# Gate stage: low parts and full copies on VectorE, one kind of sums on GpSimd, sums behind the gate units, no weight slot left out

## The reference

```python
def rmsnorm(x, w):
    xf = x.astype(jnp.float32)
    y = xf * lax.rsqrt(jnp.mean(xf * xf, axis=-1, keepdims=True) + EPS)
    return (y * w.astype(jnp.float32)).astype(x.dtype)

def first_block(x, ...):
    ...
        mix = jnp.concatenate([att, ssd, gdn], axis=-1) @ w_out[l]
        x = x + rmsnorm(mix, post_mix_norm[l])
        h = rmsnorm(x, pre_ffn_norm[l])
        f = (jax.nn.silu(h @ ffn_w_gate[l]) * (h @ ffn_w_up[l])) @ ffn_w_down[l]
        x = x + rmsnorm(f, post_ffn_norm[l])
```

## Time and profile before

| what | value |
|---|---|
| median of 3 runs | 2189.01 us |
| time of the profiled execution | 2190.16 us |
| its span, first to last instruction | 2188.0 us |
| mean granted TensorE clock | 0.983 |
| TensorE busy | 2077.9 us (95%) |
| VectorE busy | 1291.4 us (59%) |
| ScalarE busy | 952.2 us (44%) |
| GpSimd busy | 991.2 us (45%) |
| the gate stage touched here | about 656 to 745 us |
| the 20 groups of seven | about 730 to 1111 us |

### The profile page before, as it was taken

One profiled execution on the slowest core, in us unless ns is written; L12 is line 12 of the kernel. 1 busy time (PEld: TensorE's weight loads), 2 busy tenths in 40 slices (PEclk: granted clock), 3 DMA queues, 4 the chain that ended last, 5 costly groups with the idle time before them and its releaser, 6 DMA issues. The chain is left out here.

```text
span 2188.0 us, 30026 instructions
## 1 busy us (share of the span) xinstructions
PE 2077.9 (95%) x10677; PEld 1752.7 (80%) x10685; DVE 1291.4 (59%) x1872; ACT 952.2 (44%) x1691; POOL 991.2 (45%) x723
## 2 busy tenths in 40 slices
PE   7999999889998999999999988889999999999997
PEld 7888877778786788888888867769998888887886
DVE  4443604867347734434379797789997864225532
ACT  4333215566224434343445654248884445444011
POOL 2333434544246688888840312210003469885344
PEclk9999999999999999999999999999999999999999
DMA  5233412353622122222244424210001111333331
GB/s 164 77 98 110 144 54 48 66 130 54 159 58 90 29 57 68 77 68 77 68 159 147 147 85 138 97 30 1 1 1 34 39 36 46 113 97 106 106 125 77
DMA packets 185892, 179.49 MB, mean 82 GB/s; under 512 B 27556, under 2 KB 147088, under 8 KB 184336
## 3 DMA queue, kind: packets, MB, share of 16 engines
q1 hardware_dynamic: 157568, 107.51, 16.9%
q10 hardware_dynamic: 19216, 46.99, 5.8%
q0 software_dynamic: 8960, 23.07, 4.8%
HBM read 150.81 MB, written 49.81 MB: 92 GB/s over the span
## 5 line engine op out<-in xcount | busy, mean ns | idle before, releaser
L1222 POOL TENSOR_SCALAR w_hi<-w_raw 128x1024 fp32r<-128x1024 f32 x67 | 76.3, 1138 | 465.6 <-issue 309.5
L1364 PE MATMUL gemm<-h_hi,w_hi 128*128 128x512 f32 x688 | 271.4, 395 | 5.5 <-POOL h_lo L1276 5.5
L1366 PE MATMUL gemm<-h_hi,w_lo 128*128 128x512 f32 x688 | 268.1, 390 | 0.0
L1365 PE MATMUL gemm<-h_lo,w_hi 128*128 128x512 f32 x688 | 267.8, 389 | 0.0
L968 POOL TENSOR_TENSOR w_lo<-wsum,w_hi 128x512 fp32r<-128x512 f32 x160 | 214.5, 1341 | 100.2 <-ACT w_hi L1841 92.1
L1841 ACT ACTIVATE w_hi<-wsum 128x512 fp32r<-128x512 f32 x171 | 108.2, 633 | 184.0 <-POOL wsum L959 97.7
L968 POOL TENSOR_TENSOR w_lo<-w_raw,w_hi 128x512 fp32r<-128x512 f32 x86 | 117.5, 1366 | 137.9 <-ACT w_hi L1841 133.5
L1225 POOL TENSOR_TENSOR w_lo<-w_raw,w_hi 128x1024 fp32r<-128x1024 f32 x67 | 166.2, 2481 | 5.6
L1446 PE MATMUL gemm<-h_hi,w_hi 128*128 128x512 f32 x416 | 162.0, 390 | 0.7 <-issue 0.7
L1448 PE MATMUL gemm<-h_hi,w_lo 128*128 128x512 f32 x416 | 161.8, 389 | 0.0
L1447 PE MATMUL gemm<-h_lo,w_hi 128*128 128x512 f32 x416 | 161.8, 389 | 0.0
(11 more groups left out here) (494 smaller groups left out, 5366.8 us busy)
## 6 DMA issues: line engine op xcount, KB each, us to landing
w_raw<-in_w_in SPq DMA_DIRECT2D x60, 512.0 KB, 4.0
down_sums<-in_ffn_w_down POOLq DMA_DIRECT2D x24, 768.0 KB, 7.2
w_raw<-in_ffn_w_gate SPq DMA_DIRECT2D x22, 512.0 KB, 4.0
w_raw<-in_ffn_w_up SPq DMA_DIRECT2D x22, 512.0 KB, 4.1
w_raw<-down_sums SPq DMA_DIRECT2D x44, 256.0 KB, 2.7
w_raw<-in_ffn_w_down SPq DMA_DIRECT2D x44, 256.0 KB, 2.9
w_raw<-in_w_out SPq DMA_DIRECT2D x16, 512.0 KB, 3.8
sig_spill<-quad ACTq DMA_DIRECT2D x5, 1024.0 KB, 3.9
```

What stands on the lines that cost most here:

```text
L1222: gp.tensor_scalar(hi[:], raw[key % 4][:], 1.0, 0.0, ALU.mult, ALU.add).then_inc(pool_hi, 1)
L1364: mm(o, hi[:, k, m], act[0][:, k, t], start=k == 0, stop=False)
L1365: mm(o, hi[:, k, m], act[1][:, k, t], start=False, stop=False)
L1366: last = mm(o, lo[:, k, m], act[0][:, k, t], start=False, stop=k == kt - 1)
```

## The change

- In `norm` (1, 0) and (1, 1) VectorE makes the low part straight from the side bank, as in the other norms, with `low` (L2275). GpSimd's low parts (L1276) and their semaphore are gone, and TensorE's gate units no longer wait for them.
- The full copies are a new item `full`: VectorE adds `h_hi` and `h_lo` in SBUF, 8 operations for the first token half, then 4 and 4 for the second, set between the sums.
- `csum` 3 is made by GpSimd, once eight sums of kinds 1 and 0 are there. ScalarE's high parts of this kind wait for a semaphore of its own.
- `csum` and `comb` 1 no longer stand ahead of the gate units' second halves but behind them, as all others. The order behind the gate units is `full` 0, kind 1, `full` 1, kind 0, `csum` 3 (GpSimd), `full` 2, kind 2, unit up 0, `csum` 4, unit up 1, `comb` 3, `comb` 4. VectorE has no work in a gate unit, so in its queue kind 1 keeps its place; ScalarE made the high parts of kind 1 ahead of the gates' silu (L1823) and makes them behind it now.
- The row sums (`rows` (0, 1)) stand behind `norm` (1, 0), and the four residuals as an item of their own behind them; before, the residuals were mixed into the norm's copies. The second store of x1 (`load` 7) stands behind the squares and the diagonals.
- `at_slot` leaves out no slot ahead of a group of seven.

```diff
--- before.py
+++ after.py
@@ -250,11 +250,12 @@
     s += [("mx", 0)] + tk("wo", (0, 0, 0), (0, 1, 0)) + [("gn", len(NORMED) - 1), ("mx", 1), ("load", 0)]
     s += tk("wo", (0, 0, 1), (0, 1, 1), (0, 2, 0), (0, 2, 1), (0, 3, 0), (0, 3, 1))
     s += tk("wo", (1, 0, 0), (1, 1, 0), (1, 2, 0), (1, 3, 0)) + [("rows", (0, 0)), ("resid", (0, 0)), ("nsq", (1, 0))]
-    s += tk("wo", (1, 0, 1), (1, 1, 1), (1, 2, 1), (1, 3, 1)) + [("rows", (0, 1))]
+    s += tk("wo", (1, 0, 1), (1, 1, 1), (1, 2, 1), (1, 3, 1))
     begin([("gate", 0), ("gate", 1)],
-          [("norm", (1, 0)), ("load", 6), ("load", 7), ("nsq", (1, 1))],
-          [("norm", (1, 1)), ("csum", 1), ("comb", 1)])
-    s += [("csum", 0), ("comb", 0), ("csum", 2), ("comb", 2), ("csum", 4), ("csum", 3), ("unit", by["up", 0]), ("unit", by["up", 1]), ("comb", 3), ("comb", 4)]
+          [("norm", (1, 0)), ("load", 6), ("rows", (0, 1)), ("resid", (0, 1)), ("nsq", (1, 1)), ("load", 7)],
+          [("norm", (1, 1))])
+    s += [("full", 0), ("csum", 1), ("comb", 1), ("full", 1), ("csum", 0), ("comb", 0), ("csum", 3), ("full", 2), ("csum", 2), ("comb", 2)]
+    s += [("unit", by["up", 0]), ("csum", 4), ("unit", by["up", 1]), ("comb", 3), ("comb", 4)]
     for p in range(1, NF // 2):
         s += [("mul", (by["gate", 2 * p], i)) for i in range(7)]
         s += [("mul", (by["up", 2 * p], i)) for i in range(7)]
@@ -426,7 +427,6 @@
             at_slot += at_slot % 2
         elif kind == "mul":
             key, width, user = j, 1, j
-            at_slot += j[1] == 0
         elif kind == "dm":
             key, width, user = ("dm",) + j, 1, ("dm",) + j
             at_slot += j == (0, 0)
...
@@ -888,10 +888,6 @@
             if q < 3:
                 return x, y, op, bsum[k][:], [cmb[q][i][:, k, :] for i in range(2)]
             return (x, y, op) + ((b21, mul_operand(5, k)) if q == 3 else (b12, mul_operand(6, k)))
-
-        def comb_source(eng, q, k):
-
-            side_consumed(eng, (("norm", (1, int(q != 1))), k + 4 * (q != 4)))
 
         def comb_low(eng, q, k):
 
@@ -1261,6 +1257,11 @@
                         pool.wait_ge(N["sq_part"], 16 + 8 * t + 4 * h + 2 * pair + 2)
                         x = acc[:, 4 * t + 2 * pair:4 * t + 2 * pair + 2, 512 * h:512 * h + 512]
                         step(gp.tensor_tensor(x, x, over(gbc2[:, 512 * h:512 * h + 512], 2), ALU.mult), "acc_gained")
+                elif kind == "csum" and j == 3:
+                    pool.wait_ge(N["comb_sum"], 8)
+                    for k in range(4):
+                        x, y, op, dst, _ = comb_of(3, k)
+                        step(gp.tensor_tensor(dst, x, y, op), "comb_sum_p")
                 elif kind == "c2":
                     (r1, t1), (r2, t2), op = pair_of(j // 4, j % 4)
                     if j == 0:
@@ -1269,11 +1270,6 @@
                     if j >= 2:
                         pool.wait_ge(N["c2_s"], j - 1)
                     step(gp.tensor_tensor(wt[j % 2][:], hF[1][:, r1, t1], hF[1][:, r2, t2], op), "c2_w")
-                elif kind == "norm" and j[0] == 1:
-                    t = slice(512 * j[1], 512 * j[1] + 512)
-                    for k in range(KD):
-                        side_consumed(pool, (it, k))
-                        step(gp.tensor_tensor(hT[1][:, k, t], hfull[:, k, t], hT[0][:, k, t], ALU.subtract), "low_ready")
                 elif kind == "pa":
                     c, z = j, j % 2
                     if c == 0:
@@ -1359,8 +1355,6 @@
                     for k in range(kt):
                         if kd in act_ready:
                             norm_consumed(pe, act_ready[kd](hf), k)
-                        if kd == ("gate", 0):
-                            pe.wait_ge(N["low_ready"], 8 * hf + k + 1)
                         mm(o, hi[:, k, m], act[0][:, k, t], start=k == 0, stop=False)
                         mm(o, hi[:, k, m], act[1][:, k, t], start=False, stop=False)
                         last = mm(o, lo[:, k, m], act[0][:, k, t], start=False, stop=k == kt - 1)
@@ -1939,8 +1933,10 @@
                     for k in range(4):
                         if j in (2, 4):
                             act.wait_ge(N["comb_add"], 4 * (j == 4) + k + 1)
+                        elif j == 3:
+                            act.wait_ge(N["comb_sum_p"], k + 1)
                         else:
-                            act.wait_ge(N["comb_sum"], 4 * (1, 0, 3).index(j) + k + 1)
+                            act.wait_ge(N["comb_sum"], 4 * (1, 0).index(j) + k + 1)
                         _, _, _, x, dst = comb_of(j, k)
                         step(af(dst[0], x, ACT.Copy), "comb_hi")
                 elif kind == "tk":
@@ -2520,14 +2516,16 @@
                     down_evict(*j)
                     if j[0] in CLOSING and j[1] > 0:
                         last_gain(j[1] - 1)
-                elif kind == "csum" and j in (0, 1, 3):
+                elif kind == "full":
+                    t = slice(512 * (j > 0), 512 * (j > 0) + 512)
+                    for k in (range(8), range(4, 8), range(4))[j]:
+                        step(v.tensor_tensor(hfull[:, k, t], hT[0][:, k, t], hT[1][:, k, t], ALU.add))
+                elif kind == "csum" and j < 2:
                     for k in range(4):
-                        comb_source(dve, j, k)
                         x, y, op, dst, _ = comb_of(j, k)
                         step(v.tensor_tensor(dst, x, y, op), "comb_sum")
-                elif kind == "csum":
+                elif kind == "csum" and j != 3:
                     for k in range(4):
-                        comb_source(dve, j, k)
                         x, y, op, dst, _ = comb_of(j, k)
                         step(v.tensor_tensor(dst, x, y, op), "comb_add")
                         if j == 2 and k > 0:
@@ -2570,14 +2568,7 @@
                     for k in range(KD):
                         b = side_product(dve, (it, k))
                         g0 = 64 + 8 * stage + k
-                        if stage == 1:
-                            hi_count[0] += 1
-                            dve.wait_ge(N["hi_ready"], hi_count[0])
-                            step.frees(v.tensor_scalar(hfull[:, k, t], b[:], cols[:, g0:g0 + 1], None, ALU.mult), (it, k))
-                        else:
-                            low(hT[1][:, k, t], b[:], hT[0][:, k, t], (it, k), cols[:, g0:g0 + 1])
-                        if stage == 1 and hf == 0 and k % 2:
-                            residual(stage - 1, 4 + k // 2)
+                        low(hT[1][:, k, t], b[:], hT[0][:, k, t], (it, k), cols[:, g0:g0 + 1])
                 elif kind == "nk":
                     hi_count[0] += 1
                     dve.wait_ge(N["hi_ready"], hi_count[0])
```

More of the change, by code:

```diff
@@ L727, in build_program @@
             "ln_sq", "c2_w", "c2_s", "c2_hi", "c2_lo", "idr_ready", "quad_ready",
-            "low_ready", "acc_gained", "comb_sum", "comb_add", "comb_hi", "comb_lo", "w_sum", "w_quarter_hi", "t_copied", "sg_ready", "f_made", "tok_used", "ob_sq", "ob_gained")}
+            "acc_gained", "comb_sum", "comb_sum_p", "comb_add", "comb_hi", "comb_lo", "w_sum", "w_quarter_hi", "t_copied", "sg_ready", "f_made", "tok_used", "ob_sq", "ob_gained")}
         z_out = [sem(f"z_out{i}") for i in range(2)]
```

## The result

| | before | after |
|---|---|---|
| median, timed side by side (19 runs each) | 2189.96 us (2187.16 to 2195.57) | 2195.64 us (2192.68 to 2197.21) |
| span of the profiled execution | 2188.0 us | 2191.6 us |
| mean granted clock | 0.983 | 0.979 |

The ratio is 1.0015, with an interval of 1.0009 to 1.0021: 2.0 to 4.6 us slower, and within 0.5%. Why the two measures differ by 2 us is not settled. The kernel before itself spreads widely: of its 31 executions timed beside slots_only, the 16 with a mean granted clock of 0.978 or 0.979 took 2190.9 to 2195.6 us, the eight at 0.982 or 0.983 took 2188.1 to 2189.7 us. For the other kernels the ratio is given, with its interval.

What follows compares the result with a forecast made beforehand. VectorE's queue from second norm to first eviction was the bound: 678.3 + 10.7 + 50.6 + 8.7 + 1.8 + 0.8 puts the sixth product at 750.9 against 744.42, 6.5 us later. Median 2195.5 us, eight in ten 2186 to 2202.

Steps and rivals of the forecast that it cites:

- Step 1: At the second norm: it starts at 678.3 instead of 683.90, 5.6 us gained, behind 3.8 us of TensorE idle.
- Step 2: In the second norm: half clock behind the wait costs 1.6 us, counted once, here.
- Step 3: VectorE's queue: 12 more operations cost 8.7 us, contention 1.8 us more (20.9 instead of 19.1).
- Step 4: Up units and products: first product at 729.9 behind a 10 us wait, second at 737.9, 5.3 us late.
- Step 5: Slots ahead of groups of seven: weights may start one product (2.72 us) sooner, gaining and costing nothing; later stages shift unchanged.
- A: Rival at the gate stage: TensorE-bound, VectorE's work covered, sixth product 11.1 us earlier, 2177.9 us; chance 0.06.
- B: Rival in VectorE's queue: less contention, 9.7 us instead of 20.9, 2184.3 us; up to +3 us, chance 0.2.
- C: Rival at the products: half clock through four products from 737.9, +15.3 us, 2204.3 us; chance 0.05.
- D: Rival in VectorE's queue: more contention, GpSimd working without a break, +13.7 us, 2202.7; chance 0.05 with its second form.
- D's second form: VectorE's queue: contended operations wait for GpSimd's whole instruction, 1.29 us instead of 0.97, +11.5, 2200.5; chance 0.05 together.
- E: Rival at the slots: a weight late by a queue's order, 0.5 us in each of 20 groups, 2205.5 us; chance 0.03.

Runs made afterwards that it cites:

- slots_only: The kernel before with one edit: no slot is left out ahead of any group of seven; ratio 1.0014 (1.0005 to 1.0023).
- warm: The changed kernel with 14 idle identity matmuls in TensorE's wait ahead of the second norm; ratio 1.0009 (1.0000 to 1.0019).
- merged_slots: The kernel before with no slot left out ahead of the second block's twelve merged groups alone; ratio 0.9990 (0.9981 to 0.9999).
- four_more: The changed kernel with four full copies of the second token half made twice on VectorE; ratio 1.0039 (1.0026 to 1.0053).
- after_skip: The changed kernel with the left-out slot put back; ratio 1.0028 (1.0018 to 1.0038).
- scalar_full_order: As scalar_full, with unit up 0 ahead of the fifth kind of sums and up 1 ahead of the fourth; ratio 1.0004 (0.9995 to 1.0013).
- scalar_full: The kernel before with full copies by ScalarE, low parts by VectorE, and no slot left out in the second block; ratio 1.0004 (0.9995 to 1.0012).
- store_later: scalar_full_order with ScalarE's second x1 store moved behind the second half's squares; ratio against the kernel before 0.9986 (0.9977 to 0.9994).
- sums3_vector: The changed kernel with GpSimd's fourth kind of sums back on VectorE; ratio 1.0014 (1.0005 to 1.0022).

## Why the prediction was right

- **Step 1, the second norm.** Forecast 678.3 behind 3.8 us of wait; measured 678.2 (in the time of the kernel before) behind 3.58. The residuals take 1.31 us each with steps (5.25 for four), and the last square starts at 671.58, 0.1 us behind the last residual.
- **Step 2, the clock.** The half clock came, its size was too small: 2.7 us (warm) instead of 1.6. The third norm, from which I took 1.6, ran at 0.50 for its first 3.5 us; this one did so for 5.5 us (676.21 to 681.70). Either way it costs about half the stretch. That the wait of 2.89 us left full clock was one execution's word: merged_slots has 0.50 behind the same wait. The step's sentence that the half clock is counted once, in the norm, held for the sum: at the products the clock cost nothing, since the second and the sixth product still wait for VectorE (2.17 and 0.64 us).
- **Step 3, VectorE's queue.** Forecast 61.1 us, measured 60.66. Without contention the queue is 50.6 - 19.1 + 8.7 = 40.2, so contention is 20.5 us, forecast 20.9. That four sums on GpSimd gain nothing was right: they cost 0.9 to 1.0 us, forecast 1.0. That an operation more in this queue is not hidden was right too: four_more, 2.7 us for four.
- **Step 4.** First product behind a wait of 10.04 us, forecast 10. In time of before it is 731.0 (forecast 729.9), second 738.1 (737.9), sixth 751.5 (750.9). For the sixth the difference is that of step 2 less 0.4 of step 3. The second came nearly on time for another reason: the four fifth sums took 5.77 us, not 6.8. The wait ahead of it was 2.17 us and not the 5.3 that the sum has, as half clock stretched the first product to 4.9 us.
- **Step 5, the slots.** Wrong. I looked at TensorE's waits in the first block's groups alone and gave nothing to the twelve groups of the second, where TensorE had three waits for VectorE's high part, GpSimd's low weights and VectorE's sum. It is 1.75 us there (after_skip, merged_slots). "The later stages shift as they stand" failed as well: near 2006 us 0.9 us of it is lost, as the single wait there is followed by more half clock. The slots also would have cost some 4 us in the gate stage with the old order (slots_only), which the change's own order hides; this I did not see either.
- **Sum.** 6.5 + 1.1 (clock) - 0.4 (queue) is 7.2 for the stage, 7.1 measured. Less 0.5 (half clock between 1308 and 1455 us) and 1.75, and with 0.9 lost again (slots), it is 5.6 in the trace; the medians say 5.7, the ratio 2.0 to 4.6 us. So the 6.5 us were too much by every measure, and by the ratio's interval clearly so. That the median of 2195.64 us falls on the forecast of 2195.5 is luck: the side-by-side median of the kernel before is 0.95 us above the one I started from, and the clock's 1.1 us and the slots' 0.9 us have opposite signs. That the kernel before loses up to 1.25 us to half clock in some executions at the same stage, as in merged_slots, would explain a value below the trace's; it is only argued.
- **Rivals.** A and B would have needed contention gone: it is 20.5 us. C: half clock behind the second product's start lasted to about 740 us, and 0.64 us of wait were left ahead of the sixth. D: pairs of 128x512 operations cost 0.97 us each and not 1.29, since a pair takes 1.70 us and 0.69 + 1.29 would be 1.98: they overlap by some 0.3 us. The mechanism of D's second form is not refuted by this, only its price. The operation at 699.54 stood beside a GpSimd instruction of 128x1024 that ended at 701.76 (699.05 + 2.71); it took 2.77 us, and 0.55 of its own 0.69 us came behind that end. The Trainium skill, "SBUF — State Buffer", section "Who interferes with whom", says that a VectorE instruction with two SBUF inputs contends with a GpSimd instruction that reads SBUF; the trace agrees (1.67 us beside GpSimd, 0.69 alone). E: no wait in a later group, the opposite of its sign.

The change as a whole brings the second norm 5.7 us forward. Half clock takes 2.7 of that; the other 3.0 did reach the end, as VectorE's queue starts at the norm's end. It pays with 12 operations (8.7 us) and 1.4 us of contention in the very queue that sets the stage. The slots gain 1.75 us in the second block and lose 0.9 of it in this trace.

## What to carry to other kernels

Before work is moved between engines, find the queue that sets the stage and count its operations: here 5.7 us gained ahead of it were worth 3.0, and twelve more operations in it cost 8.7. Ask what stands beside work that is moved to GpSimd: four sums of 0.725 us left VectorE, and four of its operations with two SBUF inputs took 0.97 us more each. Where a queue's contention stands can matter more than how much there is (slots_only: a shorter queue, a longer stage). A store in a compute engine's queue waits here for its data and holds up what stands behind it: moving that one line shortened the stage by 2.9 us (+1.6 to -1.3).

## What the runs showed of the hardware

- VectorE's 128x512 operations with two SBUF inputs take 1.67 us beside GpSimd's 128x512 operations and 0.69 alone. Those that read a PSUM bank never took longer, beside GpSimd or not: of the 256 evictions of line 2366, all of 686 to 691 ns, 139 ran wholly beside GpSimd. A group of them, in the kernel after (ns, least, median, most):

```profile
L2366 DVE TENSOR_TENSOR ca<-m,gemm x32: 686/687/689, 748.7 to 1986.2; 128x512 f32<-128x512 f32 x32
```

- The 16 longest waits of TensorE in this stage, 3.45 to 12.89 us in ten of the twelve traces, were each followed by half clock. The shorter ones went both ways: 2.89 us by full clock in the kernel before and by 0.50 in merged_slots; 2.56 us by full clock in scalar_full_order, 2.61 us by half in scalar_full and 2.59 us by half in store_later; 1.71 and 2.31 us by full clock in sums3_vector, 2.17 us by half in the kernel after.
- Half clock of 5.5 us in a norm of 7.1 us cost 2.7 us in the end; fourteen small matmuls in the wait ahead of it gave that back.
